# A four-mixer encoder layer on one Trainium2 core: h tiles released one by one, the FFN norm applied at the PSUM exit, and norm sums partly on GpSimd

## The chip, the core and the metric

One core of a Trainium2 chip runs the whole program. The time is the device time of one launch in microseconds (us), as the median of three runs. The profile is one further execution. In the profile's rows TensorE is PE (its weight loads PEld), VectorE is DVE, ScalarE is ACT, GpSimd is POOL, and SP is the SyncE queue, which here issues all DMAs.

## The reference

```python
x = concat(RG-LRU, Mamba-2 SSD, gated DeltaNet, S5 mixers of RMSNorm(x) @ W_in) @ W_out + x
x = x + CrossAttn(RMSNorm(x), 256 memory tokens, 4 heads)
x = x + SwiGLU(RMSNorm(x))              # (silu(h @ Wg) * (h @ Wu)) @ Wd, hidden 2816
y = RMSNorm(x)                          # final norm
rmsnorm(x, g) = x * rsqrt(mean(x*x) + eps) * g
```

One layer, d = 1024, 2048 prompt tokens and 8 x 16 sample tokens, so 17 tiles of 128 tokens. All in float32.

## The kernel before, in words

**Passes and sections.** The 17 token tiles are cut into six passes: pass 0 has two tiles (256 columns), passes 1 to 5 have three (384 columns). `schedule` writes the order of all work by hand, as a list `SECS` of some 800 sections. A section is one weight block's worth of matmuls: `u` (input projection, 18 a pass), `z` (gates, tokens on the output rows; two weight halves, each a section), `w` (output projection, 8), `s` (attention scores of a head; two halves), `pt` (transposed probabilities), `vo` (values times output weights), `g` and `up` (the two FFN projections, 22 each), `d` (down projection, six blocks of four sections). `st` is a norm's sum over the partitions, by a matmul with ones. Pass p runs w, s, pt, vo, g, up, d; then u and z of pass p+2 follow. The last d block of pass p prepares pass p+2.

**Operands.** Every float32 product is made of three float32r matmuls (L381 to L383): an operand is split into a rounded part and a rest. Weights: SP loads a block into `raw`, ACT rounds it into `whi` (L760), DVE subtracts to get `wlo` (L934). Activations: the shared tile array `h` has eight tiles k of 128 channels, `hh` by ACT (L791) and `hl` by DVE (L952, L954). There is one `hh`/`hl` pair in all; kinds of h are A (input), M (memory), Y (mixers' output), C (cross attention), F (FFN). `act_prep` lets the first tile of a new h wait until the whole last section that reads the old one is done (L788 to L789).

**Norms.** For C, F and the final norm the squares of x are made by ACT (L771) and added by DVE into `acc` (L943), k by k, behind the additions to x; for A and M the same is done on the loaded tiles. Then the `st` section (PE L655, L657), a square root on ACT (L845) and a reciprocal on DVE (L1092) give `rstd`. For A, M and C `rstd` scales the matmuls' results at the PSUM exit. For F it is applied in front: DVE multiplies x by gain and rstd into `ldb` (L965), then ACT and DVE split it; `st` and all eight F tiles stand between the last `vo` (or `so`) section and the first `g`. For C the eight tiles stand behind the last `w`, and `st` in front of the first score.

**FFN.** A `g` bank is read by ACT alone: Silu into `gs` (L916). DVE multiplies `gs` by the `up` bank (L1148), ACT rounds (L921), DVE subtracts (L1048). Three PSUM banks rotate over all sections (`pe_bank`, semaphores `free`).

**The mixers.** The four recurrent mixers of a tile (a chunk) are cut by hand into 21 steps. `weave` issues on each engine, behind section i, `PLAN[i]` steps of the mixers. `spread_over_windows` spreads a pass's steps evenly over the count of its sections. GpSimd has only mixer work (masks and gates, L2351 to L2375). Every engine works in order, so a section's work on DVE stands behind the mixers' work of the section before.

**SP.** `sp_section` issues weight loads four blocks ahead, stores, h tiles (`sp_tiles`; three `ldb` slots, each waiting for the `hl` of its last user), the x of a pass at the first `w`.

## Time and profile before

| | us |
|---|---|
| median of three runs (4314.97 to 4322.67) | 4319.04 |
| profiled execution, its own time | 4323.61 |
| its span | 4321.8 |
| PE busy | 3784.8 (88%) |
| DVE busy | 2839.4 (66%) |
| ACT busy | 1805.0 (42%) |
| POOL busy | 197.7 (5%) |
| granted TensorE clock, mean share | 0.921 |

PE is the engine to look at: what it does not do in the 537 us of the span that it is idle is what other engines keep it from. Its matmuls overlap in the records, so a single duration (335 ns at 384 columns) is longer than the step from one to the next (173 ns).

### The profile page before, as it was taken

The page shows a single profiled execution, that of the slowest core. Times are in us where ns is not written, and L with a number is a line of the kernel's source. Part 1 is how long each engine was busy: PE and PEld are TensorE (multiplying, and loading weights), DVE is VectorE, ACT ScalarE, POOL GpSimd, SP SyncE. Part 2 cuts the span into 40 slices and gives each one's busy share as a digit, 9 for nine tenths or more (in the row PEclk, how much of TensorE's full clock was granted, in tenths as well). Part 3 has the DMA queues.
Part 4 walks back from the last instruction along what each step waited for, and adds up shares of the span by engine and source line. Part 5 has one row for each costly group of instructions (what it writes and reads, how often), then busy time and mean ns, then how long its engine had stood idle before and what let it go on. Part 6 is the DMA issues. An engine that isn't in the chain of part 4 may idle for free.

```text
span 4321.8 us, 63677 instructions
## 1 busy us (share of the span) xinstructions
PE 3784.8 (88%) x24260; PEld 3637.3 (84%) x24260; DVE 2839.4 (66%) x5238; ACT 1805.0 (42%) x2852; POOL 197.7 (5%) x208
## 2 busy tenths in 40 slices
PE   5688878898888999897899988899988889999998
PEld 4677876798788899887899978799978779998998
DVE  6668663377767666776765785766685666666545
ACT  4445431254444353444343444343444443434333
POOL 0000010000001000000010000000100000100000
PEclk8888978599999999998999989999999999999999
DMA  4454434344353233344233334233335223334333
GB/s 130 156 167 135 149 101 148 111 129 139 122 173 100 89 112 117 101 138 127 83 121 103 120 113 153 79 115 103 116 113 167 69 86 98 104 115 137 107 127 110
DMA packets 253055, 517.02 MB, mean 120 GB/s; under 512 B 21840, under 2 KB 151376, under 8 KB 252240
## 3 DMA queue, kind: packets, MB, share of 16 engines
q1 hardware_dynamic: 252752, 512.96, 37.6%
q8 instruction: 193, 3.16, 0.3%
q14 instruction: 110, 0.90, 0.1%
HBM read 457.94 MB, written 54.93 MB: 119 GB/s over the span
## 4 chain that ended last, share of the span: by engine, by line
PE 49%; DVE 22%; DVEq 7%; ACT 7%; DMA 5%; PEld 4%; issue 4%; ACTq 1%; SPq 0%; PEldq 0%
PE banks L381 14%; PE banks L383 13%; PE banks L382 13%; DVE wlo_sb L934 3%; DVE uc_sb L1028 2%; DVE m_p_sb L1915 2%; ACT whi_sb L760 2%; DVEq L999 2%; PE banks L1357 1%; PE banks L1363 1%; DVE rstd_sb L1092 1%; DMA x_sb<-x_t 1%; PE banks L1366 1%; PEld banks L383 1%; DVE acc_sb L943 1%
## 5 line engine op out<-in xcount | busy, mean ns | idle before, releaser
L381 PE MATMUL banks<-hh_sb,whi_sb 128*128 128x384 f32 (+2 forms) x3552 | 1227.3, 346 | 202.3 <-DVE wlo_sb L934 73.3
L934 DVE TENSOR_TENSOR wlo_sb<-raw_sb,whi_sb 128x1024 fp32r<-128x1024 f32 (+1 forms) x732 | 894.0, 1225 | 494.5 <-ACT whi_sb L760 486.2
L382 PE MATMUL banks<-hh_sb,wlo_sb 128*128 128x384 f32 (+2 forms) x3552 | 1188.7, 335 | 0.0
L383 PE MATMUL banks<-hl_sb,whi_sb 128*128 128x384 f32 (+2 forms) x3552 | 1186.4, 334 | 0.0
L381 PEld LDWEIGHTS banks<-hh_sb,whi_sb 128*128 128x128 f32 x3552 | 699.4, 197 | 250.1 <-issue 86.3
L760 ACT ACTIVATE whi_sb<-raw_sb 128x1024 fp32r<-128x1024 f32 (+1 forms) x732 | 762.0, 1051 | 161.9 <-PE banks L383 90.8
L382 PEld LDWEIGHTS banks<-hh_sb,wlo_sb 128*128 128x128 f32 x3552 | 702.0, 198 | 0.4 <-issue 0.3
L383 PEld LDWEIGHTS banks<-hl_sb,whi_sb 128*128 128x128 f32 x3552 | 699.3, 197 | 0.0
L381 PE MATMUL banks<-g_hi_sb,whi_sb 128*128 128x384 f32 (+2 forms) x1568 | 537.6, 343 | 68.6 <-DVE x_sb L1127 44.2
L382 PE MATMUL banks<-g_hi_sb,wlo_sb 128*128 128x384 f32 (+2 forms) x1568 | 524.8, 335 | 0.0
L383 PE MATMUL banks<-g_lo_sb,whi_sb 128*128 128x384 f32 (+2 forms) x1568 | 524.7, 335 | 0.0
L381 PEld LDWEIGHTS banks<-g_hi_sb,whi_sb 128*128 128x128 f32 x1568 | 312.8, 199 | 84.1 <-DVE x_sb L1127 50.1
L382 PEld LDWEIGHTS banks<-g_hi_sb,wlo_sb 128*128 128x128 f32 x1568 | 313.1, 200 | 0.0
L383 PEld LDWEIGHTS banks<-g_lo_sb,whi_sb 128*128 128x128 f32 x1568 | 312.8, 199 | 0.0
L1127 DVE TENSOR_TENSOR x_sb<-x_sb,banks 128x384 f32<-128x384 f32 (+2 forms) x400 | 201.0, 513 | 145.6 <-PE banks L383 140.5
L921 ACT ACTIVATE g_hi_sb<-gf_sb 128x384 fp32r<-128x384 f32 (+1 forms) x132 | 66.9, 507 | 541.2 <-DVE gf_sb L1148 541.2
L381 PE MATMUL banks<-whi_sb,hh_sb 128*128 128x256 f32 (+1 forms) x784 | 237.5, 303 | 62.4 <-ACTq L883 44.5
L382 PE MATMUL banks<-whi_sb,hl_sb 128*128 128x256 f32 (+1 forms) x784 | 230.6, 294 | 0.0
L383 PE MATMUL banks<-wlo_sb,hh_sb 128*128 128x256 f32 (+1 forms) x784 | 230.4, 294 | 0.0
L381 PEld LDWEIGHTS banks<-whi_sb,hh_sb 128*128 128x128 f32 x784 | 159.3, 203 | 69.4 <-issue 53.0
L382 PEld LDWEIGHTS banks<-whi_sb,hl_sb 128*128 128x128 f32 x784 | 159.2, 203 | 0.0
L383 PEld LDWEIGHTS banks<-wlo_sb,hh_sb 128*128 128x128 f32 x784 | 158.4, 202 | 0.0
(410 smaller groups left out, 4891.3 us busy)
## 6 DMA issues: line engine op xcount, KB each, us to landing
raw_sb<-w SPq DMA_DIRECT2D x624, 512.0 KB, 3.5
raw_sb<-ws_dram SPq DMA_DIRECT2D x48, 512.0 KB, 3.5
raw_sb<-vo_dram SPq DMA_DIRECT2D x48, 512.0 KB, 3.6
uc_dram<-uc_sb SPq DMA_DIRECT2D x90, 192.0 KB, 3.9
ldb_sb<-x_t SPq DMA_DIRECT2D x40, 192.0 KB, 3.2
ldb_sb<-y_dram SPq DMA_DIRECT2D x40, 192.0 KB, 2.9
x_sb<-x_t SPq DMA_DIRECT2D x5, 1536.0 KB, 8.8
y_t<-x_sb SPq DMA_DIRECT2D x40, 192.0 KB, 1.9
```

The lines of the kernel that those rows point to most:

```text
L381: eng.matmul(out, xh, yh, start=first, stop=False)
L382: eng.matmul(out, xl, yh, start=False, stop=False)
L383: return eng.matmul(out, xh, yl, start=False, stop=last)
L760: eng.activation(whi[n % SPLITS][:, 0:width], raw[n % RAWS][:, 0:width], ACT.Copy).then_inc(w_hi_done, 1)
L921: eng.activation(g_hi[:, s.a - sum(BLOCKS[:s.b]), 0:n], gf[:, s.a % 2, 0:n], ACT.Copy).then_inc(g_hi_done, 1)
L934: eng.tensor_tensor(wlo[n % SPLITS][:, 0:width], raw[n % RAWS][:, 0:width], whi[n % SPLITS][:, 0:width].bitcast(F32), ALU.subtract).then_i ...
L943: eng.tensor_tensor(a, a, sqb[:, sq % 2, 0:width], ALU.add).then_inc(sq_used, 1)
L999: eng.drain().then_inc(ev_done, 1)
L1028: last = eng.scalar_tensor_tensor(out[:, 0:n], u[:, tap:tap + n], wc, out[:, 0:n], ALU.mult, ALU.add)
L1092: eng.reciprocal(scale[:, 0:s.a + s.b], rms[:, 0:s.a + s.b]).then_inc(rstd_done, 1)
L1127: eng.tensor_tensor(out, out, bank[:, 0:wide], ALU.add).then_inc(free[(s.f + dd) % 3], 1)
L1915: eng.tensor_tensor_scan(dst[:, s * P:s * P + P], mag[:, n:n + 1].to_broadcast([P, P]), src[:, s * P:s * P + P], s5_x[:, part, n:n + 1], A ...
```

## The change

Sections: `z` and `s` sections take both weight halves in one, tile by tile; the first score head is cut into its first tile, the `st` of C, and the other tiles. The F tiles are prepared two by two in the last four `vo`/`so` sections, without rstd; the F `st` stands behind the first `g`. Each tile of a new h waits for the last section of the old one only up to that tile's own matmuls (`h_used`). Preparations stand in front of squares; in the last `w` seven C tiles are split on DVE in front of the addition. The FFN norm moves to the exit: DVE multiplies the `g` bank by rstd, ACT applies Silu in place, GpSimd multiplies by rstd once more (the factor that belongs to `up`), then DVE multiplies with the `up` bank. For the final norms and the A norms of passes 2 to 5 GpSimd makes the squares and adds them (`pool_sum`), and an `ldb` slot also waits for that. Mixer steps are spread by columns of matmul work instead of by sections, and the step of the per-token scalars gets one more place. The Y tiles' loads stand in front of the weights in their section; x of passes 1 to 4 is loaded at a `z` section earlier.

```diff
 def score(h):                                        # in schedule
-    return [Sec("s", p, h, half, ("ws", h, half), n if half == 0 else 0, hi=hc, ni=ni) for half in range(2)]
+    src = (("ws", h, 0), ("ws", h, 1))
+    if h:
+        return [Sec("s", p, h, 0, src, n, hi=hc, ni=ni)]
+    first = [Sec("s", p, h, 0, src, 1, hi=hc, ni=ni), Sec("st", p, P if p == 0 else 0, tiles(p), nf=1, ni=ni)]
+    return first + ([Sec("s", p, h, 1, (), n - 1, hi=hc, ni=ni)] if n > 1 else [])
...
-        out.append(Sec("st", p, cols(p), 0, nf=1, ni=nf))
-        out[-1].preps = preps("F", p, hf, nf)
+        spread(out[-4:], preps("F", p, hf, nf))
...
+                if t == 0:
+                    out.append(Sec("st", p, cols(p), 0, nf=1, ni=nf))
...
-            s.squares = [(fin, 2 * s.b), (fin, 2 * s.b + 1)]
+            s.sums = [(fin, 2 * s.b), (fin, 2 * s.b + 1)]
...
 def spread_over_windows():
-        for j in range(n):
-            plan[at[j * len(at) // n]] += 1
+        size = [dense_columns(i) for i in at]
+        total, done, j = sum(size), 0, 0
+        for i, c in zip(at, size):
+            done += c
+            while j < n and (j + 1) * total <= (n + 1) * done or j < n and i == at[-1]:
+                plan[i] += 1
+                j += 1
...
-CHUNK_SECTIONS, SAMPLE_SECTIONS, SCALAR_SECTIONS, N_SETUP = 21, 25, 3, 16
+CHUNK_SECTIONS, SAMPLE_SECTIONS, SCALAR_SECTIONS, N_SETUP = 21, 25, 4, 16
...
 def pe_columns(eng, i, s, n):
+                if H_LAST[s.hi] == i and k < KD - 1:
+                    last.then_inc(h_used, 1)
...
 def pe_stats(eng, s):
-            eng.wait_ge(sq_used, SQ_COUNT[s.ni])
+            if s.ni in SUM_COUNT:
+                eng.wait_ge(sum_done, SUM_COUNT[s.ni])
+            else:
+                eng.wait_ge(sq_used, SQ_COUNT[s.ni])
...
 def act_prep(eng, item):
-            if item.k == 0 and item.hi:
+            if item.hi and item.k < KD - 1:
+                eng.wait_ge(h_used, (KD - 1) * (item.hi - 1) + item.k + 1)
+            elif item.hi:
                 eng.wait_ge(full, H_FILLS[item.hi - 1])
...
 def act_unit(eng, s):
+            if s.kind == "g":
+                out = gs[:, s.a % 2, 0:cols(s.p)]
+                eng.activation(out, out, ACT.Silu).then_inc(g_gated, 1)
+                return
...
 def dve_norm_tail(eng, s):
+            dve_preps(eng, [item for item in s.preps if item not in before_adds(s)])
             for ni, k, sq, count in s.squares:
                 dve_square(eng, ni, k, sq, count, cols(s.p))
-            dve_preps(eng, s)
+        def before_adds(s):
+            return s.preps[:-1] if s.kind == "w" else []
...
 def dve_unit(eng, s):
+            if s.kind == "g":
+                eng.tensor_tensor(gs[:, s.a % 2, 0:n], bank[:, 0:n], scale[:, 0:n], ALU.mult).then_inc(g_scaled, 1)
+                eng.drain().then_inc(free[s.f % 3], 1)
+                return
...
+        def pool_sum(eng, src, ni, k, width):
+            a = acc[:, ni % 2, 0:width]
+            if k == 0:
+                eng.wait_ge(full, ST_FILL[ni - 2] + 1)
+                eng.tensor_tensor(a, src, src, ALU.mult)
+            else:
+                sq = smix[:, 0:width]
+                eng.tensor_tensor(sq, src, src, ALU.mult)
+                eng.drain()
+                eng.tensor_tensor(a, a, sq, ALU.add)
+            eng.drain().then_inc(sum_done, 1)
+        def pool_section(eng, i):
+            unit = evicted_at(i)
+            if unit is not None and unit.kind == "g":
+                g = gs[:, unit.a % 2, 0:cols(unit.p)]
+                eng.wait_ge(g_gated, unit.ev + 1)
+                eng.tensor_tensor(g, g, rstd[:, unit.ni % 2, 0:cols(unit.p)], ALU.mult).then_inc(gs_done, 1)
+            s = SECS[i]
+            for item in s.preps:
+                if item.pn >= 0:
+                    eng.wait_ge(ld_loaded[item.ld % LDS], 16 * LD_LOADS[item.ld])
+                    pool_sum(eng, h_source(item), item.ni, item.k, h_cols(item))
+            for ni, k, pn in s.sums:
+                eng.wait_ge(x_done, x_count(s.p, 2, k))
+                pool_sum(eng, x[:, k, 0:cols(s.p)], ni, k, cols(s.p))
...
 def sp_tiles(eng, items):
+                    if last.pn >= 0:
+                        eng.wait_ge(sum_done, last.pn + 1)
...
 def sp_section(eng, i):
+            elif after_mixer(s):
+                sp_tiles(eng, s.preps[:LDS])
             sp_weights(eng, ...)
...
-            if s.kind == "w" and s.a == 0:
+            if s.kind == "z" and s.a == 0 and s.p >= 2:
+                sp_x(eng, s.p - 1)
+            elif s.kind == "w" and s.a == 0:
```

## Rows read from the trace of the kernel before

**Rows 1.** The page, part 1: busy time, share of the span, instructions.

```profile
PE 3784.8 (88%) x24260; PEld 3637.3 (84%) x24260; DVE 2839.4 (66%) x5238; ACT 1805.0 (42%) x2852; POOL 197.7 (5%) x208
```

**Rows 2.** PE's own waits; columns: us in total, times, longest us.

```profile
PE banks L381 <- DVE wlo_sb L934: 84.8, 38, 7.1
PE banks L381 <- DVE hl_sb L954: 61.2, 23, 19.7
PE banks L381 <- DVE hl_sb L952: 60.9, 33, 5.2
...
PE banks L381 <- ACTq L883: 44.5, 7, 11.2
PE banks L655 <- DVE acc_sb L943: 37.3, 14, 5.1
PE banks L1596 <- DVEq L1859: 33.7, 6, 14.6
```

**Rows 3.** Windows: start and end, length, PE, PEld, DVE, ACT, POOL busy, clock, DMA.

```profile
1990.00:2050.00 60.00, 44.53 (x306) 42.34 (x307) 47.99 (x88) 28.50 (x57) 10.02 (x11) 0.83 0.25 78
...
2126.00:2486.00 360.00, 348.47 (x2208) 340.64 (x2209) 239.02 (x380) 156.44 (x229) 22.05 (x24) 0.98 0.35 110
```

**Rows 4.** Timeline, FFN start of pass 2; columns: start us, duration us.

```profile
2119.72 1.55 PE L655 MATMUL banks<-acc_sb,ones_sb 128*128 128x384 f32 x2 [2.30 <-DVE acc_sb L943]
...
2121.92 2.55 DVE L1092 RECIPROCAL rstd_sb<-rms_sb 128x384 f32<-128x384 f32 x1 [2.25 <-ACT rms_sb L845]
...
2126.47 0.66 PE L381 MATMUL banks<-hh_sb,whi_sb 128*128 128x384 f32 x1 [5.21 <-DVE hl_sb L952]
...
2134.41 0.34 PE L383 MATMUL banks<-hl_sb,whi_sb 128*128 128x384 f32 x1
```

**Rows 5.** Timeline, a section with PE never waiting: its first and 25th matmul.

```profile
1504.16 0.34 PE L381 MATMUL banks<-g_hi_sb,whi_sb 128*128 128x384 f32 x1
...
1508.33 0.33 PE L381 MATMUL banks<-g_hi_sb,whi_sb 128*128 128x384 f32 x1
```

**Rows 6.** Timeline, start of the scores of pass 1, DVE and PE.

```profile
1326.63 4.32 DVE L954 SCALAR_TENSOR_TENSOR hl_sb<-x_sb,par_sb,hh_sb 128x384 fp32r<-128x384 f32 x8
...
1344.01 5.11 DVE L1915 TENSOR_TENSOR_SCAN m_p_sb<-mag_sb,s_x_sb,m_p_sb 128x128 f32<-128x128 f32 x8
...
1351.82 0.55 PE L381 MATMUL banks<-whi_sb,hh_sb 128*128 128x256 f32 x1 [6.83 <-ACTq L883]
```

**Rows 7.** Groups of instructions by shape: count, busy us, mean ns, idle before.

```profile
L934 DVE TENSOR_TENSOR wlo_sb<-raw_sb,whi_sb 128x1024 fp32r<-128x1024 f32 x720 | 878.7, 1225 | 482.8 <-ACT whi_sb L760 475.1 <-issue 0.8
...
L943 DVE TENSOR_TENSOR acc_sb<-acc_sb,sqb_sb 128x384 f32<-128x384 f32 x140 | 78.5, 561 | 35.6 <-ACT sqb_sb L771 18.7 <-issue 6.5 <-ACTq L1775 3.7
...
L916 ACT ACT_TABLE_LOAD x60 | 77.0, 1283 | 1.1
...
L916 ACT ACTIVATE gs_sb<-banks 128x384 f32<-128x384 f32 x110 | 54.0, 491 | 161.5 <-PE banks L383 161.0
...
L2364 POOL TENSOR_TENSOR m_decs_sb<-m_dec_sb,mixc_sb 128x512 f32<-128x512 f32 x16 | 20.5, 1283 | 2.4
L2375 POOL TENSOR_TENSOR m_ytm_sb<-m_tx_sb,mixc_sb 128x256 f32<-128x256 f32 x17 | 16.2, 955 | 418.5 <-ACT m_tx_sb L1672 418.5
```

**Rows 8.** Timeline, last d sections of pass 2 into u of pass 4.

```profile
2469.62 0.44 PE L381 MATMUL banks<-g_hi_sb,whi_sb 128*128 128x384 f32 x1 [0.81 <-DVE g_lo_sb L1048]
...
2497.77 0.69 PE L381 MATMUL banks<-hh_sb,whi_sb 128*128 128x384 f32 x1 [4.91 <-DVE hl_sb L954]
...
2500.07 1.48 PE L655 MATMUL banks<-acc_sb,ones_sb 128*128 128x384 f32 x2
```

**Rows 9.** Timeline, GpSimd and DVE side by side.

```profile
873.49 1.34 POOL L2362 TENSOR_TENSOR m_dec_sb<-m_dec_sb,mixc_sb 128x512 f32<-128x512 f32 x1 [0.19 <-issue]
874.98 1.29 POOL L2364 TENSOR_TENSOR m_decs_sb<-m_dec_sb,mixc_sb 128x512 f32<-128x512 f32 x1
...
875.03 2.31 DVE L934 TENSOR_TENSOR wlo_sb<-raw_sb,whi_sb 128x1024 fp32r<-128x1024 f32 x1
```

More of the change, by code:

```diff
@@ L112 @@
     squares: list = field(default_factory=list)
+    sums: list = field(default_factory=list)
     after: int = 0
@@ L179, in stage_b @@
     def stage_b(p, hy):
[L180 removed]
+        out = [Sec("w", p, d, 0, (("w", WO + d),), 1, hi=hy) for d in range(KD)]
         hc, ni = new_h("C", p), new_norm("C", p)
@@ L290, in schedule @@
                     x.sq, sq = sq, sq + 1
+        sums = []
+        for ni, k in s.sums:
+            sums.append((ni, k, pn))
+            pn += 1
+        s.sums = sums
         if s.kind in ("u", "k"):
@@ L833, in act_second, with act_exp @@
                     eng.drain().then_inc(uc_ready, 1)
+        def act_exp(eng, s):
+            if s.a < 2:
+                end = Q_END[min(s.p + 1, NP - 1)]
+                eng.wait_ge(uc_stored[0], stored(end, 0))
+                eng.wait_ge(uc_stored[1], stored(end, 1))
+            else:
+                eng.wait_ge(full, PT_FILL[s.p, s.a - 2] + 2)
+            first = score_tiles(s)[0]
+            for j in score_tiles(s):
+                o, at, bank = s.a % 2 * 3 + j, prompt_at(s.p)[0] // P + j, (s.f + j - first) % 3
+                eng.wait_ge(s_max, S_COUNT[s.p, s.a, s.b] + j - first + 1)
+                eng.activation(pr[:, o, :], banks[:, bank, 0:MEM], ACT.Exp, bias=soft[:, o, 1:2],
+                               scale=score_c[:, at:at + 1], accum_out=soft[:, o, 2:3])
+                eng.drain().then_inc(s_exp, 1)
+                eng.drain().then_inc(free[bank], 1)
         def act_section(eng, i):
```

288 lines of the change are left out of this document (144 added, 144 removed).

## The prediction

> **What bounds the kernel now.** I read the page first: PE is busy 88% of the span, DVE 66%, ACT 42%, GpSimd 5% [rows 1]. So time can come from two places, PE's idle time (4321.8 - 3784.8 = 537 us) and slow matmuls after it. Second, the list of PE's own waits, which says who ends them [rows 2]: rests of h from L954 (61.2 us) and L952 (60.9), banks freed by the scores' exit (44.5), norm sums (37.3), token scalars (33.7), rests of weights (84.8). The first four kinds and the scalars, 237.6 us, are what the change is about; the weights' 84.8 are not, and 19.7 us of L954's are the very first load, which stays. Third, windows by stage [rows 3]: inside the FFN of a pass PE is busy 348.47 of 360 us at clock 0.98 and DVE 239 of 360, so nothing is to be won there and something can be lost; around the scores PE is busy 44.53 of 60 at clock 0.83. The waits sit at the seams between stages.
>
> **FFN start (6 seams).** Now PE waits 2.30 us for the sum, then 5.21 us for `st`, square root, reciprocal (2.55) and the first F tile, and its first g section runs from 2126.47 to 2134.6, 8.1 us, because the tiles trickle and the clock is low [rows 4]; a section that never waits takes 1508.33 - 1504.16 = 4.17 us [rows 5]. Loss: 2.3 + 5.2 + 3.9 = 11.4 us. After: the eight tiles are ready but for the last two, which need the last additions; each is then 0.6 on ACT and 0.6 on DVE, 2 to 2.5 us with the addition, while PE has 3.1 us of work on k = 0 to 5. What is late next: the norm itself. Two squares and two additions end some 5 us behind the last `vo`, then `st` 0.7, table load 1.3 and square root 0.6, reciprocal 2.55 [rows 4], exit 0.6: g's bank is free at about 10.8 us, and PE wants it for the second g at 9. I keep 2.5 us of loss. Gain 8.9 x 5, and about 6 in the narrower pass 0: **-50 us**. DVE also sheds the 48 multiplications of L965, a gain in its own load alone.
>
> **Scores' start (6 seams).** Today DVE splits eight C tiles in one piece, 4.32 us, behind the last `w`; then the reciprocal and mixer steps follow, and PE waits 6.83 us for a bank that only the scores' exit frees [rows 6]. After the change seven of the eight stand in front of the last addition, in time in which DVE waits for PE anyway. DVE reaches the scores' exit 4.3 us earlier, and `st` behind the first tile hides some 1.4 us of the sum's wait: (4.3 + 1.4) x 5 plus a little: **-30 us**. Bounds: 0 (mixer steps fill what is freed) and -57 (all of the 44.5 us, and six times 2).
>
> **Token scalars.** One more step between DVE's chain and PE's use of it is about one section more, 5 us, against waits of 33.7 us over six [rows 2], of which one alone is 14.6: **-20 us**, bounds 0 and -33.7. **Y tiles.** Of L952's 60.9 us about 34 are the FFN starts (5.21 at full width and a few short waits in the trickle, less in pass 0); 27 are Y, 4.5 a seam. Tiles may now be overwritten during the last z, and the loads go first in SP's section, but only three `ldb` slots hold y, so the other five still trickle: 2 us a seam, **-10 us** (0 to -25). The earlier load of x ends idle time of DVE, not of PE: 0.
>
> **Clock.** In the stretch around the scores the clock is 0.83 against 0.98 in the FFN [rows 3]: 60 x (1 - 0.83/0.98) = 9 us lost a pass. With two thirds of the idle time gone I take back 4 of it, five times: **-20 us** (0 to -45; at the FFN starts it is already in the 8.1 us).
>
> **GpSimd's new work.** 80 tiles of squares (32 of A, 48 of the final norms), ten of them with one instruction, 70 with two: 150. Plus 132 gate multiplications: 282 instructions. No row has one at 384 columns; at 256 GpSimd takes 955 ns, at 512 1283 ns [rows 7]. I take the middle, 1.12 us, as neither is nearer: 316 us, so GpSimd goes from 198 to about 510 us busy, 12%. DVE loses 70 additions of 0.56 us [rows 7] and the 48 of L965, at some 0.54 like L954's (4.32 / 8 [rows 6]); it gets 132 exits, at 0.55 like L943's, of two operands: +73 - 39 - 26, about even. ACT loses 80 squares.
>
> **End of the FFN into u (4 seams, passes 0 to 3).** Here the sums are dense: GpSimd has two A tiles and two final tiles a section, 4 x 2.4 = 9.6 us (two instructions of 1.12 and a start of 0.1 to 0.15 us each, as between GpSimd's two in a row [rows 9]), while PE needs 3.1 us for one of these d sections (18 matmuls of 4.17 / 24 us) and its mixer steps. Today it is DVE that is late: from the first d section to `st` take 2500.07 - 2469.62 = 30.5 us, with PE waiting for A's last tiles (4.91 us the longest) [rows 8]. After: twelve tiles follow the first addition to x before the A `st` may run, 12 x 2.4 = 29 us from about 2472 (2469.62 + 1.6 for the first bank + 0.6 for the addition), so `st` at 2501: GpSimd simply takes DVE's place. Also a slot of `ldb` is not free before its sum is made, and the eighth A tile waits for it. **0 us**, bounds -7.4 a seam (4.91 and two shorter waits go) and +12 a seam (each instruction 1.28 us and held by DVE), so -30 to +48.
>
> **FFN gate (132 times).** The new chain behind g is DVE 0.55, table load 1.28 in about half of the cases (60 for 132), Silu 0.49 [rows 7], GpSimd 1.12, with drains 3.2 us; `up` needs it one section (4.17 us) after g, so in a quiet stretch it is hidden, and a bank is wanted only two sections later still. But DVE now stands in its queue, before it can exit `up`, and with it the weights' rests and mixer steps behind it. DVE is busy two thirds of the time there, so most of this goes into idle time; I take 4 us a pass: **+25 us**; bounds 0 and 132 x 1.12 = +148.
>
> What the two engines do to each other shows in the trace: while GpSimd works from 874.98 on for 1.29 us, DVE's subtraction of 1024 columns, two operands in SBUF, takes 2.31 us [rows 9], where its mean is 1.22 [rows 7]. So each of the 282 may cost DVE up to 2.31 - 1.22 = 1.09 us. The Trainium skill, "SBUF — State Buffer", section "SBUF: two separate sides", says that this pair of ports is an exclusive lock held for the whole instruction; by it alone, with every one of the 282 on the path, this would be the slower case below. The Trainium skill, "GPSIMD Engine Reference", section 4.1, names VectorE for elementwise work on a tile, as GpSimd is about two times slower with two inputs; by that rule the change takes the wrong engine, which is the same slower case. The trace agrees on the ratio: 1283 / 512 = 2.5 ns a column against 561 / 384 = 1.5 [rows 7].
>
> **Tail.** In pass 5 nothing hides the final sums: eight tiles at 2.4 us less one instruction, 18 us, against four sections of 3.1 us plus some 2 now: **+5 us**.
>
> Sum: -50 - 30 - 20 - 10 - 20 + 0 + 25 + 5 = **-100 us** on the profiled execution's 4323.6, 4223.6. The runs' median stands 4.6 us under that execution, so **4219 us**.
>
> **The rivals.** *The lock decides (slower).* Place: FFN and its last block. If DVE is the engine that PE waits for, each GpSimd instruction lengthens the path by the row's 1.09 us, not a tenth of it: 132 x 1.09 = +144 in place of 25, and the four seams at +12 = +48. Sum: -130 + 144 + 48 + 5 = +67, 4386 us. It decides from the point where DVE's share in the FFN window, 66% now, passes about 85%. For it: DVE has scans of the mixers in one piece of 5.11 us, behind which PE already waits [rows 6]. Against it: banks give two sections, 8 us, of slack, and 66% + 22 x (0.55 + 1.1)/360 is 76%. *Only the FFN seam gives.* DVE's mixers refill what the other seams free: -50 - 10 + 25 + 5 = -30, 4289 us. For it: the scores' wait ends on DVE, and the rows have mixer scans in front. *All named waits go.* With balanced mixer steps also a third of the weights' waits: -237.6 + 19.7 + 15 - 28 - 20 + 25 + 5 is about -220, so 4099 us; for it the small idle share in the other stages, against it the ladder of ever next late things. That the change does not do what it says I give nothing: all its waits are in the diff.
>
> **The numbers.** Forecast 0.6, slower by the lock 0.14, FFN seam alone 0.16, all gone 0.1. Forecast's own range by its bounds: 4140 to 4290. Eight in ten: 4125 to 4320, which takes in the seam-only case and leaves out most of the lock's and some of the best case. Faster or slower counts from 0.2%, 9 us, about what a measurement of this kernel can tell from no change. Faster: 0.82; within: 0.04; slower: 0.14.
>
> **What would show it.** Right: L952's waits on PE under 25 us, `acc` waits under 15, the F start's first g section near 4.2 us, clock mean over 0.93, GpSimd near 500 us busy. Wrong: DVE over 75% with PE waiting for L1127, wlo or `up` inside the FFN window (PE under 340 of 360 us); PE waiting longer for A's `st`, with POOL as releaser; the wait for the scores' banks still near 40 us.

## The result and the profile after

The changed kernel takes 4336.48 us (median of eight runs, 4332.64 to 4346.36) against 4316.92 us for the kernel before (eight runs of the same session, 4313.68 to 4327.95). The ratio is 1.0044, with a 95% interval of 1.0032 to 1.0057: slower by 0.44%, some 19 us, where 4219 us were forecast. The profiled execution took 4333.73 us, its span is 4331.9 us, 10.1 us over that of before.

The page's busy line of the changed kernel, and PE's own waits (us in total, times, longest). Line numbers are those of each kernel: L1009, L1011, L992, L1183, L912, L1111 and L1001 are here what L952, L954, L934, L1127, L883, L1057 and L943 are in the kernel before, except that the F tiles have moved from the first to the second.

```profile
PE 3753.5 (87%) x24250; PEld 3618.8 (84%) x24250; DVE 2886.1 (67%) x5252; ACT 1762.9 (41%) x2776; POOL 486.7 (11%) x490
```

```profile
PE banks L415 <- DVE wlo_sb L992: 94.7, 40, 7.8
PE banks L415 <- DVE x_sb L1183: 70.6, 25, 7.9
PE banks L415 <- DVE hl_sb L1011: 69.0, 24, 18.9
PE banks L415 <- DVE hl_sb L1009: 66.2, 22, 13.5
PE banks L415 <- DVEq L1111: 35.7, 8, 5.7
PE banks L415 <- DVE g_lo_sb L1102: 26.1, 8, 5.7
PE banks L709 <- POOLq L1227: 23.3, 3, 9.8
...
PE banks L1677 <- DVEq L2077: 5.1, 1, 5.1
```

Against [rows 1, 2]: PE is idle 578 us where it was 537, although three of the five named kinds of wait did shrink: sums on DVE (37.3 us) are nearly gone (0.5), the scores' exit (44.5) is down to 16.1, the token scalars (33.7) to 5.1. The rests of h did not: L1011 has 69.0 us for 61.2, and L1009 (Y tiles) 66.2 us, more than Y and F together took at L952 before, x additions 70.6 instead of 45.9, and GpSimd appears with 23.3. One more kind is new at this size: banks that the exit of the transposed probabilities frees on DVE, L1111, with 35.7 us, where the kernel before has

```profile
PE banks L667 <- DVEq L1057: 12.4, 7, 2.6
PE banks L381 <- DVEq L1057: 4.3, 7, 1.0
```

The five named kinds together fell by 81 us (237.6 to 156.9), and PE's idle time rose by 41. DVE is no busier than 67%.

Where the time went is best read from one pass cut at the same events in both kernels, here pass 2. The cuts are ends of DVE instructions: first `w` addition, first and last `vo` addition, exit of the second and of the 22nd `up`, last `d` addition, next first `w` addition. Windows of the kernel before (start and end, length, PE, PEld, DVE, ACT, POOL busy, clock, DMA share, GB/s):

```profile
1971.60:2076.24 104.64, 84.52 (x584) 81.19 (x584) 77.23 (x169) 50.57 (x93) 11.03 (x12) 0.90 0.30 94
2076.24:2118.24 42.00, 38.99 (x263) 37.91 (x261) 29.84 (x54) 12.32 (x26) 0.00 (x0) 1.00 0.30 93
2118.24:2152.75 34.51, 26.58 (x146) 23.22 (x147) 27.42 (x43) 12.10 (x18) 0.00 (x0) 0.85 0.17 55
2152.75:2468.42 315.67, 306.67 (x1948) 301.69 (x1947) 201.87 (x318) 135.91 (x196) 22.05 (x24) 0.99 0.36 114
2468.42:2495.11 26.69, 21.10 (x139) 19.32 (x137) 22.13 (x38) 14.65 (x28) 0.00 (x0) 0.94 0.36 121
2495.11:2649.58 154.47, 132.09 (x799) 127.07 (x800) 106.38 (x194) 64.64 (x96) 0.00 (x0) 0.91 0.46 144
```

The same stretches of the changed kernel:

```profile
1997.46:2103.34 105.88, 87.33 (x579) 84.87 (x578) 71.25 (x160) 48.79 (x90) 11.05 (x11) 0.90 0.31 98
2103.34:2141.92 38.58, 37.61 (x252) 36.57 (x253) 29.72 (x49) 17.25 (x27) 0.98 (x1) 1.00 0.30 97
2141.92:2162.57 20.65, 20.65 (x129) 20.38 (x129) 16.70 (x25) 9.63 (x17) 2.03 (x2) 1.00 0.34 107
2162.57:2493.28 330.71, 314.78 (x2009) 309.51 (x2008) 226.96 (x365) 134.91 (x200) 47.03 (x47) 0.98 0.33 108
2493.28:2519.76 26.48, 21.08 (x139) 20.44 (x138) 24.32 (x29) 10.80 (x18) 19.37 (x19) 0.87 0.41 130
2519.76:2678.39 158.63, 126.07 (x772) 120.03 (x772) 106.60 (x191) 61.09 (x90) 9.05 (x9) 0.90 0.44 136
```

The third row is the FFN start, that of [rows 4]: 34.51 us became 20.65, PE never idle, clock 1.00 instead of 0.85; part of the gain is mixers' work that left the stretch (129 matmuls for 146). The sum of F, behind the first g, now waits for nothing:

```profile
2146.63 0.81 PE L709 MATMUL banks<-acc_sb,ones_sb 128*128 128x384 f32 x2
```

The fourth row of both is the FFN: 15 us longer; PE is busy 8 us more (2009 matmuls for 1948: mixers' steps were moved in) and idle 15.9 us for 9.0. The last, from the last `d` to the next `w`, is 4 us longer although PE has 6 us less to do. The same cuts summed over all passes, in us (duration, and PE's idle time in brackets; here a wait is counted whole in the stretch in which it ends, so that single stretches differ from the windows above, and the 14 us behind PE's last matmul are left out):

| stretch | before | after | difference |
|---|---|---|---|
| start to first w of pass 0 | 529.9 (136.3) | 553.6 (151.5) | +23.7 |
| first w to first vo, six | 589.1 (112.6) | 556.9 (100.0) | -32.2 |
| vo and so | 459.7 (48.1) | 429.1 (42.2) | -30.6 |
| last vo to second up: FFN start | 196.7 (49.4) | 122.3 (2.2) | -74.4 |
| second to 22nd up: FFN | 1761.1 (56.3) | 1848.0 (93.2) | +86.9 |
| 22nd up to last d | 136.8 (21.4) | 130.5 (26.3) | -6.3 |
| last d to next w, five | 632.1 (96.8) | 668.4 (141.2) | +36.3 |
| last d to the end | 16.5 (2.1) | 23.0 (7.7) | +6.5 |

Durations also carry mixers' work that changed its stretch; idle time doesn't. So the FFN start gave 47 us of idle time, and the scores and `vo` 18 more. Against that stand 37 us more in the FFN, 5 behind it, 44 ahead of the next `w`, 15 before pass 0 and 6 at the end.

### The profile page after: what moved, and what is told of

The parts are those of the page before. It is cut to its first block, busy times and chain, and to the rows that moved or that the text cites. A ratio compares the mean times of both kernels' runs of the same rounds, so it can differ in the third digit from the quotient of the medians.

```text
span 4331.9 us, 63980 instructions
## 1 busy us (share of the span) xinstructions
PE 3753.5 (87%) x24250; PEld 3618.8 (84%) x24250; DVE 2886.1 (67%) x5252; ACT 1762.9 (41%) x2776; POOL 486.7 (11%) x490
## 4 chain that ended last, share of the span: by engine, by line
PE 47%; DVE 24%; DVEq 7%; DMA 6%; ACT 6%; issue 4%; PEld 2%; POOLq 1%; ACTq 1%; SPq 1%; PEldq 0%; POOL 0%
PE banks L415 13%; PE banks L416 12%; PE banks L417 12%; DVE wlo_sb L992 4%; DVE uc_sb L1082 3%; DVE m_p_sb L2020 2%; ACT whi_sb L814 2%; DVEq L1053 2%; DMA uc_dram<-uc_sb 2%; PE banks L1459 1%; PE banks L1465 1%; DVE hl_sb L1011 1%; PE banks L1468 1%; DVE m_p_sb L1990 1%; PE banks L764 1%
## 5 line engine op out<-in xcount | busy, mean ns | idle before, releaser
L992 DVE TENSOR_TENSOR wlo_sb<-raw_sb,whi_sb 128x1024 fp32r<-128x1024 f32 (+1 forms) x732 | 907.9, 1245 | 405.4 <-ACT whi_sb L814 396.0
L415 PE MATMUL banks<-g_hi_sb,whi_sb 128*128 128x384 f32 (+2 forms) x1568 | 540.2, 345 | 129.4 <-DVE x_sb L1183 70.6
L1234 POOL TENSOR_TENSOR gs_sb<-gs_sb,rstd_sb 128x384 f32<-128x384 f32 (+1 forms) x132 | 128.5, 973 | 1943.2 <-ACT gs_sb L862 1943.2
L415 PE MATMUL banks<-whi_sb,hh_sb 128*128 128x256 f32 (+1 forms) x784 | 242.9, 310 | 93.2 <-DVEq L1111 35.7
L1183 DVE TENSOR_TENSOR x_sb<-x_sb,banks 128x384 f32<-128x384 f32 (+2 forms) x400 | 200.3, 512 | 136.6 <-PE banks L417 131.4
L862 ACT ACTIVATE gs_sb<-gs_sb 128x384 f32<-128x384 f32 (+1 forms) x132 | 66.9, 507 | 322.0 <-DVE gs_sb L1039 322.0
```

Source lines behind the costliest of these rows:

```text
L415: eng.matmul(out, xh, yh, start=first, stop=False)
L862: eng.activation(out, out, ACT.Silu).then_inc(g_gated, 1)
L992: eng.tensor_tensor(wlo[n % SPLITS][:, 0:width], raw[n % RAWS][:, 0:width], whi[n % SPLITS][:, 0:width].bitcast(F32), ALU.subtract).then_i ...
L1183: eng.tensor_tensor(out, out, bank[:, 0:wide], ALU.add).then_inc(free[(s.f + dd) % 3], 1)
L1234: eng.tensor_tensor(g, g, rstd[:, unit.ni % 2, 0:cols(unit.p)], ALU.mult).then_inc(gs_done, 1)
```

## The experiments

All ratios are to the kernel before in the same session, with 95% intervals; the changed kernel stands at 1.0044. "us" against it is the difference of ratios times 4320. The intervals are 0.2 to 0.5% wide, so that a difference of under some 8 us between two kernels is hardly told apart.

**x of a pass back at its first w.** In the profile of the changed kernel the last z section ahead of pass 2 reads so (timeline of SP, ACT and PE; start us, duration us):

```profile
1969.33 0.56 SPq L1321 DMA_DIRECT2D x_sb<-x_t  x1
1969.94 0.65 SPq L2548 DMA_DIRECT2D y_dram<-m_lb_sb  x1
1977.21 1.28 SPq L1280 DMA_DIRECT2D ldb_sb<-y_dram  x3
1978.54 0.90 SPq L1259 DMA_DIRECT2D raw_sb<-w  x2
1979.48 7.25 SPq L1294 DMA_DIRECT2D z_dram<-uc_sb  x3
```

```profile
1985.92 0.47 ACT L939 ACTIVATE uc_sb<-banks,rstd_sb 128x256 f32<-128x256 f32 x1 [12.67 <-DMA z_dram<-uc_sb]
```

```profile
1987.82 0.66 PE L415 MATMUL banks<-hh_sb,whi_sb 128*128 128x384 f32 x1 [12.34 <-DVE hl_sb L1009]
```

SP issues the 1.5 MB of x at 1969.33, the mixers' last y store at 1969.94, and then stands until that store has landed, at 1977.1. Behind SP's wait are two weight loads and the z stores; ACT's third z exit waits 12.67 us for a slot of `uc` that such a store must free, the first Y tile is split behind it, and PE waits 12.34 us. That store's time to landing (last number, us) in the changed kernel and then in the one before, both ahead of pass 2; in the changed kernel the stores ahead of passes 1, 3 and 4 take 7.0 to 7.1 as well:

```profile
y_dram<-m_lb_sb SPq DMA_DIRECT2D x1, 128.0 KB, 7.2
```

```profile
y_dram<-m_lb_sb SPq DMA_DIRECT2D x1, 128.0 KB, 1.8
```

```diff
-            if s.kind == "z" and s.a == 0 and s.p >= 2:
-                sp_x(eng, s.p - 1)
-            elif s.kind == "w" and s.a == 0:
-                if s.p in (0, NP - 1):
-                    sp_x(eng, s.p)
+            if s.kind == "w" and s.a == 0:
+                sp_x(eng, s.p)
```

> The changed kernel, but x of every pass is loaded at its first w section again, as before the change. Theory (x in front of the y store): in the changed kernel SP issues the 1.5 MB load of x 0.6 us ahead of the mixers' last store of y, whose landing takes 7.2 us where it took 1.8 before, and y's loads, the z stores behind them in SP's queue, the exit of z on ACT and the split of the first Y tile all follow it. Then the waits of PE for L1009 fall from 66 us to 25 or less, the store of y lands in 2 to 3 us, and the kernel is 25 to 45 us faster than the changed one, about 4300 us. Rival (the y loads in front of the z stores in SP's queue, or the mixers' later last step, are what costs): the waits for L1009 stay over 50 us and the time within 8 us of the changed kernel's 4336.

4328.32 us, 1.0014 (1.0003 to 1.0026): 13 us faster than the changed kernel, half of what the theory wanted. The store lands in 1.8 us again, but the waits for L1009 fall only from 66.2 to 47.1 us:

```profile
PE banks L415 <- DVE hl_sb L1009: 47.1, 16, 8.5
```

```profile
1973.53 0.47 ACT L939 ACTIVATE uc_sb<-banks,rstd_sb 128x256 f32<-128x256 f32 x1 [8.71 <-DMA z_dram<-uc_sb]
```

Theory right in the mechanism, not in the size: the exit still waits 8.71 us for `uc`, with y's loads and two weights issued ahead of the z stores. The Trainium skill, "DMA: Bandwidth & Descriptors", section "Queues, rings and completion order", says that descriptors of one issuing queue are consumed in ring order on each DMA engine; by that rule the small store has to wait for the x load issued before it. The trace agrees: 7.2 us behind the x load, 1.8 us without it.

**Stores first.** The z stores of the last z section ahead of its two weight loads, on top of that kernel:

```diff
+            late = after_mixer(s) and s.kind == "z"
+            if not late:
                 sp_weights(...)
...
+            if late:
+                sp_weights(...)
```

> The changed kernel with x at the first w, and SP issues the stores of the last z section in front of that section's two weight loads. Theory (the z stores wait behind 1 MB of weights, so that the third exit of z on ACT and the first Y tile behind it are late): the waits for L1009 fall from 47 us to 30 or less and the time by 5 to 15 us against the kernel with x at w (1.0014 of before). Rival (SP then stands at the third exit until the section is over, and the weights of the first w are late in its place): waits for L992 rise from 99 us to over 120, and the time by 5 to 25 us.

4316.12 us, 0.9993 (0.9977 to 1.0009), 9 us less, at the edge of what can be told; L1009 falls to 36.6 us, not quite to the 30 of the theory, the longest wait from 8.5 to 4.2, and L992 doesn't rise (94.8). So the order in SP's queue is most of what was left: in the kernel before, Y's waits were 30 us. In the best kernel, below, it does nothing:

> The same order of stores and weights in the best kernel (0.987 of before). Theory: 3 to 10 us faster. Rival: 5 to 25 us slower, with later weights.

0.9874 (0.9851 to 0.9898), neither theory.

**The mixers' window one section shorter**, with x at the first w:

```diff
-    windows.append((0, first, len(secs) - 1))
+    windows.append((0, first, len(secs) - 2))
...
-            windows.append((p + 1, first, len(secs) - (1 if p + 2 < NP else 8)))
+            windows.append((p + 1, first, len(secs) - (2 if p + 2 < NP else 8)))
```

> The changed kernel with x loaded at the first w, and the mixers' window one section shorter, so that their last step stands ahead of the first z section as before the change; y's loads keep their place. Theory (with the x load moved alone, SP still waited for y's store at the head of the last z section, so that two weight loads and the z stores were issued behind y's loads, and the third exit of z waited 8.7 us for its uc slot): now SP waits for nothing there, the waits for L1009 fall from 47 to 30 us or less, and the time by a further 8 to 20 us against the kernel with x at w (1.0014 of before), so to 0.997 to 1.000 of before. Rival (the 1.6 MB that are issued ahead of the z stores hold them, wherever the mixers' last step is): L1009 stays over 40 us and the time within 6 us of that kernel.

4353.6 us, 1.0071 (1.0050 to 1.0091). L1009 did fall, to 33.0 us, but the kernel is 25 us slower: the second to the 22nd up exit takes 1874 us in place of 1851. The theory on the y wait holds nearly, that on the time is wrong. Each shift of the window moves all later steps, which the theory left out; that this is the 25 us was not shown by itself, but waits rose in many places (L992 98.9 to 110.5, POOL 23.3 to 33.0, mixers' m_lg 9.1 to 22.5).

**Final norms' squares back on ACT and DVE.**

```diff
-            s.sums = [(fin, 2 * s.b), (fin, 2 * s.b + 1)]
+            s.squares = [(fin, 2 * s.b), (fin, 2 * s.b + 1)]
```

> The changed kernel, but the final norms' squares are made by ACT and added by DVE again; GpSimd keeps the A norms' sums and the gate. Theory (GpSimd's sums are late at the A and the final st): PE's waits for POOL at the st, 23.3 us in three, fall under 6 us, DVE gets 42 additions of 0.56 us more, ACT 48 squares, and the time falls by 10 to 25 us. Rival (DVE's own load decides at the end of the FFN): DVE is late where GpSimd was, acc waits come back at 15 us or more, and the time is within 8 us or up to 15 us longer.

4309.66 us, 0.9970 (0.9957 to 0.9982): 32 us faster, more than expected (the two profiled executions differ by 21). In the changed kernel GpSimd's last sum and the `st` behind it, at the end of pass 4, read:

```profile
3898.36 0.99 POOL L1226 TENSOR_TENSOR acc_sb<-acc_sb,smix_sb 128x384 f32<-128x384 f32 x1
```

```profile
3899.45 1.65 PE L709 MATMUL banks<-acc_sb,ones_sb 128*128 128x384 f32 x2 [9.80 <-POOLq L1227]
```

At the end of pass 2, the seam of [rows 8], PE no longer waits 4.91 us for A's tile but twice for DVE, which now works beside GpSimd; with the squares back the first of these two waits is 2.90 us:

```profile
2513.83 0.69 PE L415 MATMUL banks<-g_hi_sb,whi_sb 128*128 128x384 f32 x1 [5.40 <-DVE x_sb L1183]
2524.10 0.53 PE L415 MATMUL banks<-hh_sb,whi_sb 128*128 128x384 f32 x1 [2.28 <-DVE hl_sb L1011]
```

With the squares back no wait of PE for POOL is left (23.3 us with GpSimd's sums), and DVE's sums take PE 9.1 us. Both sums back on DVE wasn't tried: with two `sqb` buffers ACT's third square of a section would wait for an addition that DVE makes only behind the next mixers' step.

**Mixers' steps spread evenly.**

```diff
-        size = [dense_columns(i) for i in at]
-        ...
+        for j in range(n):
+            plan[at[j * len(at) // n]] += 1
```

> The changed kernel, but the mixers' steps are spread evenly over the count of a window's sections, as before the change. Theory (the spreading by columns packs the steps of pass 0 into the u sections between the M and C sums, where PE's idle time rose by 27 us): the start of the scores of pass 1, 30 us later than before the change, comes 15 to 30 us earlier, and the time falls by as much; the later passes stay within 3 us each. Rival (the balance helps the later passes): they lose 3 to 6 us each to waits for weights and banks, and the sum is within 8 us or slower by up to 20 us.

4310.09 us, 0.9970 (0.9958 to 0.9982), 32 us faster, a little more than the 15 to 30 of the theory; the first w addition comes at 526.3 us instead of 553.6. Why, the timeline of PE at the stage of u of pass 1 shows. Window 0 has 50 steps, and by columns six of its sections get two:

```profile
409.75 1.11 PE L1430 MATMUL banks<-mixc_sb,m_tqk_sb 128*128 128x128 f32 x4 [4.96 <-ACT m_dec_sb L1742]
...
420.52 2.08 PE L1511 MATMUL banks<-m_cht_sb 64*128 64x128 f32 x16 [7.09 <-ACT m_cht_sb L1747]
```

No section's matmuls stand between these two steps, so PE waits 4.96 us in the first and 7.09 in the second for what ACT makes of the step before.

**One step behind each section**, still by columns:

```diff
+        for i in at:
+            if plan[i] == 2:
+                free_ = [k for k in at if plan[k] == 0]
+                if free_:
+                    plan[min(free_, key=lambda k: abs(k - i))] += 1
+                    plan[i] -= 1
```

> The changed kernel, its mixers' steps still spread by columns, but where a section had two steps behind it, one goes to the nearest section that has none: nine of the 50 places of window 0 move, and one or two steps of the later windows. Theory (two steps behind one section leave PE no dense work between them, so that it waits for the other engines' part of the step): nearly all that the even spreading brought comes back, 20 to 35 us faster than the changed kernel, 0.9963 to 0.9998 of before, with the first w addition near 526 us instead of 554. Rival (the spreading by columns as such costs, through the later passes' places): within 10 us of the changed kernel.

4322.17 us, 1.0001 (0.9988 to 1.0014): 19 us faster by the ratio, a little under what was expected, and the first w addition at 528.2 us. The doubled steps are the loss before pass 0, 25 of 27 us in the profiles. Behind the first w addition the changed kernel and the evenly spread one take as long (3778 us), this one 9 us more, so that it stays 13 us behind the even spreading. Set beside the three-part kernel below:

> The changed kernel with x at the first w, the final squares on ACT and DVE, and the spreading by columns with one step a section; to be set beside the kernel with the same two parts and the even spreading (0.993 of before). Theory (once no section has two steps, both spreadings are worth the same within the chance of the places): 0.990 to 0.996. Rival (columns are better in the later passes, as the change meant): below 0.989.

4279.68 us, 0.9908 (0.9887 to 0.9928), as the theory had it, and 10 us below the three-part kernel (0.9930), which the intervals can't tell apart. But the pair before it, 1.0001 by columns with one step each and 0.9970 evenly, differs by 13 us the other way round, outside its intervals. So neither spreading is better as such once no section has two; where the steps fall in the rest of the kernel is worth some 10 us either way.

**Without GpSimd's gate multiplication**, and then **without both factors**:

```diff
-                eng.activation(out, out, ACT.Silu).then_inc(g_gated, 1)
+                eng.activation(out, out, ACT.Silu).then_inc(gs_done, 1)
```

> The changed kernel without GpSimd's multiplication of the gate by rstd (132 instructions of 0.97 us); silu goes straight to DVE's product. This leaves out the factor rstd of the up projection. Theory (the gate's chain holds DVE in its queue in front of the up exit, and the lock lengthens DVE's work beside it): PE's waits for L1102 and L1183 fall from 97 us to about 60, the mean of L992 from 1.245 to 1.225 us, and the time by 15 to 40 us. Rival (two sections of slack hide it): within 8 us.

4331.96 us, 1.0025 (1.0012 to 1.0037): 8 us for 132 instructions, the rival's bound and hardly more than none. The theory is wrong: L1183 stays at 70.2 us, L1102 at 26.0.

```diff
-            if s.kind == "g":            # in dve_unit
-                eng.tensor_tensor(gs[...], bank[:, 0:n], scale[:, 0:n], ALU.mult).then_inc(g_scaled, 1)
+            if s.kind == "g":            # in act_unit
+                bank = bank_in(eng, s.f)
...
+                eng.wait_ge(up_done, done - 1)
+                eng.activation(gs[...], bank[...], ACT.Silu).then_inc(gs_done, 1)
```

> The changed kernel with neither factor rstd in the FFN: ACT applies silu straight from the g bank as before the change, and DVE and GpSimd lose 132 multiplications each. This leaves the FFN norm's rstd out. Theory (it is DVE's exit of the g bank that costs, because the bank now comes free only behind the mixers' steps in DVE's queue, and not GpSimd's multiplication, whose removal brought 8 us): in passes 1 to 3 PE's idle time from the second to the last up exit falls from 16 us to about 9, and the whole kernel is 25 to 45 us faster than the changed one, 0.994 to 0.999 of before. Rival (the idle time there comes from the mixers' steps at their new places): it stays over 13 us a pass and the time within 12 us of the kernel without the second gate (1.0025).

4305.9 us, 0.9958 (0.9941 to 0.9974), 29 us below the kernel without the gate. The FFN of pass 2 in the changed kernel has 15.9 us of idle PE; here, by the window of the same stretch, 13.7:

```profile
2156.82:2484.48 327.66, 314.00 (x2015) 308.81 (x2013) 214.37 (x345) 136.10 (x200) 27.49 (x27) 0.99 0.33 108
```

Over six passes it is 93.2 us, 87.7 without the gate, 73.5 without both, and 56.3 before the change. So the exit on DVE is most of what the norm costs, as expected in time, while the idle time didn't fall to 9: 17 of the 37 us stay. I put them down to the steps' new places, which no run here separates. In pass 5, which has no mixers, the FFN takes 247.6 us before and 247.4 after: exit and gate cost nothing where no mixers' step stands in front of them.

**ACT empties the g bank** (and GpSimd multiplies twice), in the best kernel:

```diff
+                eng.activation(gs[...], bank[...], ACT.Copy).then_inc(g_out, 1)       # ACT, at g
+                eng.tensor_tensor(g, g, rstd[...], ALU.mult).then_inc(g_scaled, 1)    # GpSimd
+                eng.activation(out, out, ACT.Silu).then_inc(g_gated, 1)               # ACT, a section later
```

> The best kernel so far (four parts undone, 0.987 of before), with the g bank emptied by ACT: ACT copies it into gs, GpSimd multiplies by rstd, ACT applies silu one section later, GpSimd multiplies once more. DVE loses 132 multiplications, GpSimd gets 132 more. Theory (DVE's exit costs what its removal together with the gate's brought, 29 us against the kernel without GpSimd's gate): 12 to 28 us faster than that kernel, 0.981 to 0.984 of before. Rival (the longer chain is late for the up exit, or the 132 further GpSimd instructions hold DVE): same within 6 us or slower by up to 30 us, with PE's waits for DVE's up exit or L1097 above 90 us.

4276.88 us, 0.9899 (0.9886 to 0.9912): 12 us slower than that kernel, not faster. The rival's sign, but not its waits of over 90 us: PE waits for the `up` exit nowhere, L1103 (L1097 of the best kernel) has 16.5 us after 9.6, and the x additions 62.4 after 66.3. The FFN of passes 1 to 3 is 5 to 6 us longer each; why stays open.

**C tiles split behind the last addition.**

```diff
-            return s.preps[:-1] if s.kind == "w" else []
+            return []
```

> The changed kernel, but DVE splits the C tiles behind the last addition to x instead of seven of them in front. Theory (DVE is late at the last w anyway, behind a mixers' step of 6 us and the weights, so that the seven splits only push the last addition, and with it the eighth tile and the sum, back by their own 3.8 us, and what the change won at the bank exit it lost here): the time from the first w addition to the first vo addition, 106 us a pass, stays within 2 us and the kernel within 8 us of the changed one (1.0044 of before). Rival (the early splits do save 4.3 us a seam as predicted): 15 to 25 us slower than the changed kernel.

4331.18 us, 1.0023 (1.0012 to 1.0034), 9 us faster, just more than can be told. DVE at the end of the last w sections of pass 2 in the changed kernel, and then PE:

```profile
2017.91 0.18 DVE L1937 TENSOR_SCALAR tk_sb<-tk_sb 128x24 f32<-128x24 f32 x1
...
2024.27 0.15 DVE L1958 TENSOR_SCALAR tsc_sb<-tk_sb 128x12 f32<-128x12 f32 x1
...
2026.32 0.54 DVE L1166 TENSOR_TENSOR x_sb<-x_sb,banks 128x384 f32<-128x384 f32 x1
...
2029.54 3.79 DVE L1011 SCALAR_TENSOR_TENSOR hl_sb<-x_sb,par_sb,hh_sb 128x384 fp32r<-128x384 f32 x7
2033.24 0.55 DVE L1166 TENSOR_TENSOR x_sb<-x_sb,banks 128x384 f32<-128x384 f32 x1
```

```profile
2030.29 0.55 PE L415 MATMUL banks<-whi_sb,hh_sb 128*128 128x256 f32 x1 [4.72 <-DVE hl_sb L1011]
```

The seam is that of [rows 6], in the next pass. The step of the token scalars holds DVE from 2017.9 to 2024.4, with two additions to x still to come; before the change four came behind it. So x is late, ACT's C tiles are late, and then seven splits push the last addition, the eighth tile and the sum back by 3.79 us. The first w to the first vo takes 105.9 us in pass 2 as against 104.6 before. The edit leaves PE's waits as they are (L1011 71.4 us, L1111 35.8): the C tiles are late in either order. In the best kernel the same edit does nothing:

> The best kernel (four parts undone, 0.987 of before) with the C tiles split behind the last addition as well. Theory (the seven splits in front delay the last addition by 3.8 us a seam, of which 1 to 2 us reach PE): 3 to 10 us faster, 0.985 to 0.9865. Rival (with DVE less late the early splits do help): 3 to 15 us slower.

0.9871 (0.9847 to 0.9895).

**All F tiles behind the last vo.**

```diff
-        spread(out[-4:], preps("F", p, hf, nf))
+        spread(out[-1:], preps("F", p, hf, nf))
```

> The changed kernel, but all eight F tiles are prepared behind the last vo or so section instead of two by two behind the last four; the norm stays at the exit. Theory (the seam's gain, 13.4 us a full pass from the last vo addition to the second up exit, is made of the norm's wait that is gone and of the tiles' early preparation): the stretch grows from 20.6 to 23 to 26 us, and the kernel is 12 to 30 us slower than the changed one, 1.007 to 1.011 of before. Rival (tiles behind the last section are ready in time, one by one, and only the norm's wait mattered): within 8 us.

4345.31 us, 1.0065 (1.0050 to 1.0080): 9 us slower, at the edge of what can be told, the stretch 23.8 us for 20.6. Between both theories. Of the 13.9 us that a full pass gained at the FFN start, the early tiles give 3.2, and 2.2 of these are paid in the `vo` stretch in front (38.6 us, 36.4 here); the other 10.7 are the norm's place together with the mixers' steps that left.

**Token scalars with three places**, as before the change:

```diff
-CHUNK_SECTIONS, SAMPLE_SECTIONS, SCALAR_SECTIONS, N_SETUP = 21, 25, 4, 16
+CHUNK_SECTIONS, SAMPLE_SECTIONS, SCALAR_SECTIONS, N_SETUP = 21, 25, 3, 16
```

(and one `yield` less on PE, ACT, DVE and GpSimd).

> The changed kernel with three places for the token scalars, as before the change. Prediction's term: 20 us of waits come back, the named wait for DVE at the token matmul rises from 5 us to about 30, and the kernel is 10 to 30 us slower than the changed one. Rival (the scalars' chain then only waits where it waited, and one place less moves all later steps): within 8 us, though the named wait rises.

4351.58 us, 1.0068 (1.0047 to 1.0090): 10 us slower, which the intervals hardly tell from none; the named wait is back at 31.9 us in five. So 27 us of this wait are worth some 10 us of time, half of the prediction's term. This edit, too, moves all later steps.

**Parts together.** x at the first w, final squares, even spreading; then the shorter window as a fourth:

> The changed kernel with three parts undone together: x at the first w, the final norms' squares on ACT and DVE, and the mixers' steps spread evenly. Alone they brought 13, 32 and 32 us. Theory (they act at different places and add up): 0.982 to 0.987 of before, about 4255 us. Rival (x and the plan both act on the same seam from z to w, and the final sums' waits are taken up by the next late thing): 0.988 to 0.993.

4292.94 us, 0.9930 (0.9913 to 0.9947).

> As the kernel with three parts undone, and with the mixers' window one section shorter. Theory: a further 8 to 15 us below that kernel, about 0.980 to 0.984 of before. Rival: within 5 us of it.

4267.68 us, 0.9872 (0.9852 to 0.9892). Three parts that alone gave 13, 32 and 32 us give 49 together: the rival. The fourth gives 25 more, above the 8 to 15 of its theory, where in the kernel by columns the same edit cost 25. This is the best version, 74 us below the changed kernel and 55 below the one before. A last edit to it, no mixers' step behind the last three w:

```diff
-    return not (s.kind == "w" and s.a == KD - 1 or ...
+    return not (s.kind == "w" and s.a >= KD - 3 or ...
```

> The best kernel so far (four parts undone), with no mixers' step behind the last three w sections (before: only the last). Theory (a mixers' step on DVE in front of the last additions makes the C tiles late, 4.7 us of PE a pass): PE's waits for L1006 fall from 50 us to under 35 us and the time by 8 to 20 us. Rival (the steps only go elsewhere and DVE's late additions do not bind): within 6 us.

4298.33 us, 0.9951 (0.9939 to 0.9962): 34 us slower, against both theories; L1006 (the L1011 of this kernel) didn't fall (53.4), and the FFN of passes 1 to 3 grew by 7 us each, while the waits for the exit of the transposed probabilities went from 32.6 to 42.6 us and those for the `up` rests from 9.6 to 23.6. Which of the moved steps does that stays open.

## Why the prediction was wrong

**FFN start (-50): right in mechanism, about right in size.** The first g never waits; the stretches shrank by 74 us, 47 of them idle time, and the rest is the clock, which rose there from 0.85 to 1.00, and mixers' matmuls that left. What was kept for the late norm (2.5 us a pass) wasn't needed.

**Y tiles and x (-10 and 0): this step failed.** "The earlier load of x ends idle time of DVE, not of PE: 0" priced the load where it ends and not what is queued behind it. It delayed the y store by 5.4 us and with it y's loads, two weights, the z stores and ACT: 13 us of the kernel, and the stores behind the weights 9 more. Y's waits, 30 us of L952's 60.9 by the trace (forecast 27, to fall by 10), became 66.

**The spreading: no term at all.** The sum has nothing for it, though it decides what stands behind every section; only the fastest rival booked a gain, 28 us of the weights' waits, and these rose from 84.8 to 94.7. It measured +32 us, 19 of them from sections with two steps.

**End of the FFN into u (0): this step failed.** "GpSimd simply takes DVE's place" held for the `st` of A in passes 1 to 3 alone, where no wait for POOL shows; PE waits there for DVE instead. The final sums alone cost 32 us: the A `st` waits 5.8 us in pass 0, the final `st` 9.80 in pass 4 and 7.71 in the tail, and DVE's splits beside GpSimd take twice their time (below). The bounds (-30 to +48) were for passes 0 to 3; pass 4, whose final sums nothing covers either, had no term.

**Scores' start (-30): this step failed.** The wait for the scores' bank went as said (44.5 to 16.1 us), but others took its place in the same stretches: 28.6 us for C tiles (L1011), where there was none, and the 35.7 us of L1111. The seven splits stood behind a late DVE and in front of the last addition; that costs 9 us, hardly more than can be told. The second kind reads so in pass 2, DVE and then PE:

```profile
2076.16 5.20 DVE L2020 TENSOR_TENSOR_SCAN m_p_sb<-mag_sb,s_x_sb,m_p_sb 128x128 f32<-128x128 f32 x8
```

```profile
2083.42 0.58 PE L415 MATMUL banks<-whi_sb,hh_sb 128*128 128x256 f32 x1 [5.71 <-DVEq L1111]
```

A whole score head wants a bank that DVE frees only behind the mixers' scan. In all, L1111 has 38.3 us here and L1057 16.7 before; the even spreading leaves 32.6, so the new sections have a part in it, but no run has the merged heads alone. The stretches of passes 1, 2, 3 and 5 are 1 to 2 us longer. Those of passes 0 and 4 are 22.9 and 15.2 us shorter, 15.5 and 7.2 of it PE's busy time, mixers' work that left them.

**FFN gate (+25): 37, right in sign, wrong in place.** 8 us for GpSimd's 132 multiplications, 29 for DVE's exit, which was booked as "about even" in DVE's load (which rose by 47 us in all). Work put into DVE's idle time is free only while no bank waits behind a mixers' step.

**Token scalars (-20): 10. Tail (+5): 6.5. Clock (-20): 0**; the mean is 0.922 after 0.921, as the idle time did not fall. GpSimd's busy time, 487 us, was forecast as 510. Of the prediction's own signs, `acc` and GpSimd's load came as for "right"; L952's waits (under 25) came out at 66 and the clock (over 0.93) at 0.922.

The slower rival had the sign but not the mechanism: by it the 132 multiplications would cost 144 us, and they cost 8. Its condition, DVE above 85% in the FFN, isn't met: 226.96 of 330.71 us in pass 2, 69%. The terms as measured one by one don't add up to the whole (the three parts show that), so no single sum of them is claimed. The larger fault is of method: the gains were read off PE's list of waits, each as if the work behind it stood still, while the change moved all the mixers' steps; the named waits fell by 81 us and others rose by more.

## What to carry to other kernels

In a kernel whose side work is laid out between sections, any edit that changes the number of sections moves all of that work; here one and the same edit gave 25 us in one kernel and cost 25 in another, and a second one cost 34; fix the layout first, or try several, before judging an edit of ten. Don't put two dependent steps behind one section. Before a large load is moved forward, look at which small transfers its queue issues next and who waits for them; and before an exit moves to a busier in-order engine, look at the longest piece in front of it, not at the engine's share.

## What the runs showed of the hardware

Of the DVE instructions measured here beside GpSimd, those with both inputs in SBUF are held, as in [rows 9], and the x additions, with one in PSUM, aren't. End of pass 3's FFN in the changed kernel, DVE and then GpSimd:

```profile
3192.51 1.23 DVE L1183 TENSOR_TENSOR x_sb<-x_sb,banks 128x384 f32<-128x384 f32 x2
3193.87 2.07 DVE L1011 SCALAR_TENSOR_TENSOR hl_sb<-ldb_sb,par_sb,hh_sb 128x384 fp32r<-128x384 f32 x2
3195.86 2.02 DVE L992 TENSOR_TENSOR wlo_sb<-raw_sb,whi_sb 128x1024 fp32r<-128x1024 f32 x1
```

```profile
3193.41 1.01 POOL L1226 TENSOR_TENSOR acc_sb<-acc_sb,smix_sb 128x384 f32<-128x384 f32 x1
...
3195.67 1.12 POOL L1226 TENSOR_TENSOR acc_sb<-acc_sb,smix_sb 128x384 f32<-128x384 f32 x1
3196.97 1.59 POOL L1224 TENSOR_TENSOR smix_sb<-x_sb 128x384 f32<-128x384 f32 x1 [0.18 <-issue]
...
3199.91 0.83 POOL L1224 TENSOR_TENSOR smix_sb<-ldb_sb 128x384 f32<-128x384 f32 x1 [0.18 <-issue]
```

The two splits at 3193.87 take 2.07 us for 2 x 0.58, and L992 2.02 for its usual 1.22. GpSimd's square at 3196.97 takes 1.59 us for 0.83: it starts inside L992 and ends 0.68 us after L992 does. Of the x additions, over the trace 53 of them stand beside a GpSimd instruction by 0.2 us or more and take 0.518 us, the 347 others 0.511. For L1011 it is 33 at 1.196 against 119 at 0.579, for L992 48 at 1.559 against 684 at 1.222. That makes 33 x 0.62 + 48 x 0.34 = 37 us of DVE's time in the whole span, mostly where the sums and the A splits meet. The Trainium skill, "SBUF — State Buffer", section "SBUF: two separate sides", names DVE instructions with two inputs in SBUF, beside those in a two-port mode, as the ones that lock a GpSimd instruction which reads SBUF out or are locked out by it; the trace agrees for two inputs in both directions, and says nothing here on the other kind.

The mean price of a GpSimd instruction was also a little lower than read from its neighbours in [rows 7]. Groups of the changed kernel (count, busy us, mean ns):

```profile
L1234 POOL TENSOR_TENSOR gs_sb<-gs_sb,rstd_sb 128x384 f32<-128x384 f32 x110 | 111.5, 1014 | 1599.5 <-ACT gs_sb L862 1599.5
L1226 POOL TENSOR_TENSOR acc_sb<-acc_sb,smix_sb 128x384 f32<-128x384 f32 x63 | 74.2, 1178 | 9.6 <-issue 0.4
...
L1224 POOL TENSOR_TENSOR smix_sb<-ldb_sb 128x384 f32<-128x384 f32 x28 | 25.4, 906 | 5.7 <-issue 4.2 <-DMA ldb_sb<-x_t 1.5
```

At 384 columns that is 1.01 us for the gate, 1.18 for the additions and 0.91 for these squares, 1.04 over all 245 new instructions, for the 1.12 that was taken. With no such DVE instruction beside them it is 1.01 for gate and addition and 0.83 for a square, which reads one tile twice.
